# Two token sums moved into the projections, layer 2's first block sums moved behind two branch products, and first expert weight pieces asked for in another order

## The reference, cut to what matters

```python
def mixer_projections(h, w_in_l, q_norm_l, k_norm_l):
    z = jnp.einsum('bnd,de->bne', h, w_in_l)
    u_f, q_g, k_g, v_g, q_d, k_d, v_d, gates = jnp.split(z, _split_points(), axis=-1)
...
def merge_branches(u_f, o_g, o_d, gates, w_f, w_go, w_do, w_out):
    g_f, g_g, g_d = jnp.split(jax.nn.sigmoid(gates), N_BRANCHES, axis=-1)
    merged = (g_f * (fourier_mix(u_f) @ w_f)
              + g_g * (o_g @ w_go)
              + g_d * (o_d @ w_do))
    return merged @ w_out
...
    for l in range(DEPTH):
        h = modulate(rms_norm(x, norm1_g[l]), sh1, sc1)
        ...
        x = x + g1[:, None, :] * merge_branches(u_f, o_g, o_d, gates, w_fourier[l],
                                                w_gqa_o[l], w_diff_o[l], w_out[l])
        h = modulate(rms_norm(x, norm2_g[l]), sh2, sc2)
        x = x + g2[:, None, :] * moe(h, w_router, router_bias, w_e_gate[l], w_e_up[l], w_e_down[l])
```

## Time and profile before

| | us |
|---|---|
| three timed executions | 1937.16, 1942.76, 1942.72 (median 1942.72) |
| profiled execution, its own time | 1943.26 |
| its span, first to last instruction | 1941.2 |
| around the span | 2.06 |
| PE busy in the span | 1726.5 (89%) |
| DVE, ACT, POOL busy | 957.3, 718.6, 501.9 |
| TensorE clock granted, mean | 0.957 of full |

### The profile page before, as it was taken

The page is one execution under the profiler, slowest core; times in us unless marked ns, Lnnn a source line. Parts: engine busy times, 40 slices in busy tenths (PEclk is TensorE's granted clock), DMA queues, the critical chain, the costliest instruction groups (busy, mean ns, idle before and its releaser), DMA issues. The chain is left out here.

```text
span 1941.2 us, 34689 instructions
## 1 busy us (share of the span) xinstructions
PE 1726.5 (89%) x13363; PEld 1351.5 (70%) x13363; DVE 957.3 (49%) x1849; ACT 718.6 (37%) x1394; POOL 501.9 (26%) x268
## 2 busy tenths in 40 slices
PE   5999999989999987788689998888899999588893
PEld 4899866679999974222188997567899998432222
DVE  4285476785667333111283744766766652611114
ACT  4443465553433421111254434656433342211113
POOL 1303410065456302000101123201545551200004
PEclk8999999999999988999789999999999999899996
DMA  7512377823522337987442221001232340889744
GB/s 275 195 44 68 106 249 248 275 94 129 192 91 88 143 143 298 360 303 261 143 147 98 67 67 36 1 2 44 66 98 66 98 145 21 354 311 393 278 136 174
DMA packets 170647, 305.95 MB, mean 158 GB/s; under 512 B 12530, under 2 KB 123250, under 8 KB 169716
## 3 DMA queue, kind: packets, MB, share of 16 engines
q1 hardware_dynamic: 151248, 249.09, 37.1%
q10 hardware_dynamic: 13476, 33.67, 4.8%
q0 software_dynamic: 5760, 20.97, 2.9%
HBM read 517.87 MB, written 41.68 MB: 288 GB/s over the span
## 5 line engine op out<-in xcount | busy, mean ns | idle before, releaser
L2422 PE MATMUL psum<-xw,h_T 128*32 128x512 f32 x1792 | 209.3, 611 | 36.0 <-DMA xw<-w_expert 32.4
L181 PE MATMUL psum<-whi,h_hi 128*128 128x256 f32 x720 | 210.1, 292 | 0.5 <-ACT v_tok L1011 0.5
L817 POOL TENSOR_TENSOR wlo<-raw,whi 128x2048 fp32r<-128x2048 f32 x25 | 115.2, 4608 | 362.3 <-ACT whi L897 362.3
L181 PE MATMUL psum<-whi,h_lo 128*128 128x256 f32 x720 | 203.5, 283 | 0.0
L181 PE MATMUL psum<-wlo,h_hi 128*128 128x256 f32 x720 | 203.5, 283 | 0.0
L2422 PEld LDWEIGHTS psum<-xw,h_T 128*32 128x32 f32 x1792 | 53.9, 111 | 170.5 <-issue 113.5
L977 ACT ACTIVATE prob<-psum,small_stats 128x640 f32<-128x640 f32 (+1 forms) x160 | 112.0, 705 | 134.5 <-DVE small_stats L1380 134.3
L1380 DVE TENSOR_REDUCE small_stats<-psum 128x1 f32<-128x640 f32 (+1 forms) x160 | 107.3, 712 | 96.7 <-PE psum L1684 72.2
L2319 DVE TENSOR_TENSOR gated_x<-psum,sig_x 128x256 f32<-128x256 f32 x28 | 11.9, 425 | 279.9 <-ACT sig_x L2066 279.9
L181 PEld LDWEIGHTS psum<-whi,h_hi 128*128 128x128 f32 x720 | 137.5, 191 | 3.0 <-issue 1.8
L181 PEld LDWEIGHTS psum<-wlo,h_hi 128*128 128x128 f32 x720 | 137.9, 192 | 0.0
(11 more groups left out here) (375 smaller groups left out, 4108.3 us busy)
## 6 DMA issues: line engine op xcount, KB each, us to landing
xw<-w_expert SPq DMA_DIRECT2D x672, 512.0 KB
raw<-w_in SPq DMA_DIRECT2D x46, 1024.0 KB, 5.4
wm_rest<-w_mod SPq DMA_DIRECT2D x40, 1024.0 KB, 5.3
y_rows<-y_sel ACTq DMA_DIRECT2D x108, 128.0 KB, 5.2
h_sel<-h_rows ACTq DMA_DIRECT2D x22, 512.0 KB, 6.9
wm<-w_mod SPq DMA_DIRECT2D x4, 2048.0 KB, 16.1
raw<-w_out SPq DMA_DIRECT2D x8, 1024.0 KB, 5.2
h_rows<-c_zero ACTq DMA_DIRECT2D x4, 1536.0 KB, 8.9
```

The costliest lines, as they stand in the source:

```text
L181: mm = pe.matmul(dst, st, mv[q], start=start and n == 0, stop=stop and n == 2)
L817: pool.tensor_tensor(wlo[i % 2][:, :, :], raw[i % 2][:, :, :], whi[i % 2][:, :, :].bitcast(F32), ALU.subtract).then_inc(w_lo, 1)
L2422: mm = pe.matmul(psum[list_rows(q), i % 2, :], hT[i % 2][:, kc, q, :], xw[q][c][:, k * 512:(k + 1) * 512], start=(kc == 0), stop=(kc == KD ...
```

## The change

It moves instructions; none is added or removed.

A. SP stores `x_kept` after `stream(2)` instead of after `stream(4)`.

B. POOL's five steps of f_1 and f_2 stand behind `lo(3)` and ahead of `lo(6)`, the two low parts of s_1 and s_2 behind `lo(6)` and ahead of `lo(7)`. ACT's `sum_high(0)` and `sum_high(1)` stand ahead of units z(5, 1) and z(5, 3) instead of in attention steps 12 and 13.

C. Layer 2: POOL starts f_3 only when DVE has scaled the differential attention's rows (`d_3`). DVE's first four block sums and the three steps of s_4 stand behind the gate products of branch chunks 0 and 1, and s_4's low part behind that of chunk 3. ACT's `sum_high(2)` stands behind all seven `block_hi` of the first chunk. Layer 1: `sum_high(2)` stands behind `keep_diff` and ahead of the last five `block_hi`, not right behind `pw_high(0)`.

D. SP's pieces for the first expert tile: 7 at `g_pfree` 24 (before 4), 4 more at `o_full` 6, 11 at `o_full` 8 (before 18), 2 at `k_d` as before.

```diff
@@ sync
                     for i in range(2, N_WIN + (1 if first else 2)):
                         stream(i)
-                        if i == 4:
+                        if i == 2:
@@ gpsimd
+                    def first_sums():
+
+                        pool.wait_ge(n_lo, KD if first else 2 * KD)
+                        pool.wait_ge(x_moved, 16)
+                        add_up(f_1[1], f32(h_21[0]), f32(h_22[0]), ALU.add)
...
                         lo(i)
...
+                        if i == CH_KVG - 1:
+                            first_sums()
+                        if i == CH_QD + 1:
+                            for n, s in enumerate((s_1, s_2)):
+                                pool.wait_ge(a_hi, n + 1)
+                                pool.tensor_tensor(s[1], (f_1, f_2)[n][1], f32(s[0]), ALU.subtract).then_inc(a_lo, 1)
+
+                    if not first:
+                        pool.wait_ge(d_3, DH)
                     pool.wait_ge(t_o, NA)
@@ scalar
                     for n, u in enumerate(units):
+                        if u in (("z", CH_QD, 1), ("z", CH_QD, 3)):
+                            sum_high(u[2] // 2)
...
-                        if i in (12, 13):
-                            sum_high(i - 12)
...
                         pw_high(0)
-                        sum_high(2)
...
                     block_hi(n0, 0)
                     block_hi(n0, 1)
                     keep_diff()
-                    for j in range(2, 7):
-                        block_hi(n0, j)
+                    if first:
+                        sum_high(2)
+                        for j in range(2, 7):
+                            block_hi(n0, j)
+                    else:
+                        for j in range(2, 7):
+                            block_hi(n0, j)
+                        sum_high(2)
@@ vector
+                            if not first and g == 1:
+                                first_blocks()
+                            if g == (0 if first else 3):
                                 dve.wait_ge(a_hi, 4)
@@ sync, experts
+                    EARLY = [(c, 0) for c in range(N_PARTS + 1)] + [(2, 3), (3, 3)]
+                    LAST_STREAM = [(0, 2), (1, 2), (2, 1), (3, 1)]
+                    for c, q in EARLY:
+                        first_part(c, q)
+                    sp.wait_ge(o_full, KD - 2)
+                    for c, q in LAST_STREAM:
+                        first_part(c, q)
                     sp.wait_ge(o_full, KD)
```

More of the change, by code:

```diff
@@ L822, in _ @@
                             modulate_pool(pool, h_mix, kc)
[L823 to L826, removed]
                     n_step = [0]
@@ L837, in summed @@
                         pool.wait_ge(a_step, n)
[L839 to L843, removed]
-                    f32 = lambda x: x.bitcast(F32)
[L845 to L855, removed]
+                    f32 = lambda x: x.bitcast(F32)
+                    def first_sums():
+                        pool.wait_ge(n_lo, KD if first else 2 * KD)
+                        pool.wait_ge(x_moved, 16)
+                        add_up(f_1[1], f32(h_21[0]), f32(h_22[0]), ALU.add)
+                        add_up(f_1[0], f32(h_21[1]), f32(h_22[1]), ALU.add)
+                        summed(2)
+                        add_up(f_1[1], f_1[1], f_1[0], ALU.add)
+                        summed(3)
+                        add_up(f_2[1], f_1[1], f32(h_11[0]), ALU.subtract)
+                        summed(4)
+                        add_up(f_2[1], f_2[1], f32(h_11[1]), ALU.subtract)
+                    for i in range(2, N_WIN + n0):
+                        if i in (CH_KVG, CH_QD):
+                            continue
+                        lo(i)
+                        if i == CH_KVG - 1:
[6 more added lines that the diff above has]
+                        pool.wait_ge(d_3, DH)
                     pool.wait_ge(t_o, NA)
@@ L978, in exps, with sum_high @@
                                            accum_out=small[:, s, 1:2]).then_inc(t_exp, 1)
+                    def sum_high(n):
+                        s = (s_1, s_2, s_3, s_4)[n]
+                        act.wait_ge(a_step, (5, 5, SUM_STEPS, SUM_STEPS + 3)[n])
+                        act.activation(s[0], (f_1, f_2, f_3, f_4)[n][1], ACT.Copy).then_inc(a_hi, 1)
                     n_sqrt = 0
                     for n, u in enumerate(units):
+                        if u in (("z", CH_QD, 1), ("z", CH_QD, 3)):
+                            sum_high(u[2] // 2)
                         act.wait_ge(s_full, n + 1)
@@ L1040, in _ @@
                             exps(AHEAD[u])
[L1043 to L1047, removed]
                     def block_hi(n, j):
@@ L1962, in load_down @@
                                      bounds_check="skip_entire_dma").then_inc(xd_ld[h], 16)
-                    def first_down(q):
-                        for h in range(2):
-                            sp.dma_start(xw[q][N_PARTS + h][:, :], w_exp[N_PARTS + h, PER_LIST * q]).then_inc(xd_ld[h], 16)
                     def store_y(i, lists):
@@ L1977, in _ @@
                     low_ready(sp, N_STREAM - 1)
-                    for c in range(N_PARTS):
-                        for q in range(1, N_LISTS):
-                            sp.dma_start(xw[q][c][:, :], w_exp[c, PER_LIST * q]).then_inc(xw_ld[c], 16)
-                    for q in (0, 1, 3):
-                        first_down(q)
+                    rest = [(c, q) for c in range(N_PARTS) for q in range(N_LISTS)] + [(N_PARTS + h, q) for q in (0, 1, 3) for h in range(2)]
+                    for c, q in rest:
+                        if (c, q) not in EARLY + LAST_STREAM:
+                            first_part(c, q)
                     sp.wait_ge(k_d, TT)
-                    first_down(2)
+                    for h in range(2):
+                        first_part(N_PARTS + h, 2)
                     sp.wait_ge(k_t, KD)
```

25 lines of the change are left out of this document (13 added, 12 removed).

## The result

| | us |
|---|---|
| changed kernel, four executions | 1950.92, 1955.56, 1959.61, 1959.77 (median 1957.59) |
| kernel before, beside it | median 1942.22 |
| ratio, 95% interval | 1.0076 (1.0049 to 1.0104) |
| profiled execution, its own time and span | 1950.92, 1948.7 |
| PE, DVE, ACT, POOL busy | 1724.6, 954.7, 715.0, 510.4 |

What follows compares the result with a forecast made beforehand. PE, busy 89% of the span, was taken as the bound, others mattering only where it stands still. Terms -6.3 + 8.4 + 2.5 + 0.4 - 5.7 = -0.7 us gave 1942.0 us (own range 1938 to 1946; eight in ten 1932 to 1949.5).

Steps and rivals of the forecast that it cites:

- Attention: Attention with POOL's sums and low parts moved out: -5.0 us in layer 2, -1.3 in layer 1, together -6.3.
- Projections: Projections, where the moved POOL work makes DVE wait: +4.2 us a layer, +8.4 in all, bounds 0 and 17.
- The meeting of the fifth sum with one product: Projections: DVE's first product of chunk 2 waits 2.8 us for POOL; after slack of 1.1, PE loses 1.7 us.
- the second meeting: Projections: `lo(6)`, two low parts and `lo(7)` hold DVE's rotary products of rows (5,1) to (5,3); PE loses 2.5 us.
- the first rival: Projections absorb the sums, as DVE's products don't wait or slack exceeds 1.1 us: 1933.6 us, chance 0.29.
- Merge, layer 2: Layer 2's merge: PE's 4.60 us wait for `pw_lo` goes, a 5.0 us wait for POOL's low part comes: +0.4 us.
- Merge, layer 1, its start: Layer 1's merge: late `sum_high(2)` delays POOL's low parts and PE's block products: +2.5 us, bounds 0.5 and 3.5.
- Experts: First expert tile: earlier pieces let the last scatter land sooner, shortening PE's wait for `h_sel`: -2.5 and -3.2, together -5.7 us.
- the third rival: Experts stay as they were, since the scatters' own traffic sets the last landing: 1947.7 us, chance 0.10.
- The step that failed, first: Projections: SP's earlier store of `x_kept` delays two chunks of `w_in` by 12 us: counted as nothing, up to 2 us.
- The step that failed, second: Layer 1's merge: beyond the +2.5 us counted there, nothing in that layer gives anything back for it.
- the port lost at `lo(7)`: Projections: `lo(7)` takes the port ahead of row (5,2)'s last product: +7.4 us, 1949.4 us, chance 0.12.

Runs made afterwards that it cites:

- the first run: The changed kernel with the store of `x_kept` put back behind `stream(4)`, all else kept: ratio 1.0105 to the kernel before, median 1960.93 us.
- the eighth run: The kernel before with only layer 2's piece of part C (its merge) changed: ratio 0.9997 to the kernel before, -0.6 us.
- ninth run: The kernel before with layer 1's `sum_high(2)` late and, in both layers, each `pw` chunk asked for ahead of the raw chunk: ratio 1.0004.
- the sixth run: The changed kernel, in layer 1 storing `x_kept` behind `stream(3)` after ACT's small loads landed, and `sum_high(2)` right behind `pw_high(0)`: ratio 1.0010, median 1940.68 us.

## Why the prediction was wrong

The steps one by one, with what the trace of after gives:

- **Attention.** Layer 2 -4.4 of -5.0 forecast, layer 1 -0.5 of -1.3 (what runs on POOL there is `lo(11)`; layer 1 has no `lo(12)`). The mechanism held; the low parts of layer 1 gave less than those of layer 2, whose number was borrowed.
- **Projections.** Layer 1 +1.5 and +2.1 (forecast 1.7 and 2.5), layer 2 +3.8 (4.2). The meeting of the fifth sum with one product, its 2.8 us, the slack, and the second meeting all came close to what was worked out. This was the step on which the first rival stood: the products do wait. The Trainium skill's rule ("SBUF — State Buffer", "Who interferes with whom") was the right one to follow, and the rows of 2.80 and 5.84 us now show it for products with two inputs in this stage; the first run shows such waits for a `TENSOR_SCALAR` of four columns (2.57 us) and a copy (2.85) as well.
- **Merge, layer 2.** +0.3 (0.4), with a wait of 5.21 where 5.0 was forecast. Held, and the run of this piece alone agrees.
- **Merge, layer 1, its start.** +1.9 (2.5). Held.
- **Experts.** -0.8 by the run of the pieces alone, -1.6 and -1.2 in the trace of after, against -5.7. The premise failed that the pieces were in the scatters' way: in layer 2 it took 7.8 us after (1699.99 to 1707.81) and 8.6 before (1684.96 to 1693.58) from the last scatter's issue to SP's `h_sel` load, not about 6. This was the third rival. The wait for `h_sel` can't be read by itself: it fell from 5.62 to 3.08 us in layer 1 with the pieces alone, but to 2.77 and 2.03 in the eighth and ninth run too, which keep the old order, because PE had waited longer for `h_T` just ahead. The two waits together are 6.5 and 7.7 us (layers 1 and 2) in the mean of the six traces with the old order, and 5.7 and 6.4 in the mean of the eight with the new one: a gain of 0.8 and 1.3 us.
- **The step that failed, first.** "SP's earlier store of `x_kept` ... nothing, up to 2 us." I had asked only which chunks of `w_in` stand behind the store on SP's queue. The loads that suffered are issued by another engine, ACT, and DVE waits for them until 67.60 us: +7.9 in the trace, 7.6 by the run of the store alone. That row was in the trace of before with 9.95 us of waiting for `lam_in`; it is the place where layer 1's start has no slack. The Trainium skill says, in "DMA: Bandwidth & Descriptors", "Issuing engines are not separate DMA queues", that SP's and ACT's transfers go through the same engines; the trace agrees, with 12.4 us for a load that took 7.1.
- **The step that failed, second.** "Nothing in layer 1 gives anything back for it" stopped at the merge's first chunk. The delay doesn't stay 1.9 us; through SP's order of loads it puts the stage on its slower course: 5.5 us. The prediction named what waits behind POOL on PE, and not who waits for POOL's low parts on SP.

A third term was mis-sized, the experts' -5.7, which measured -0.8. With the failed steps put in, 7.9 + 5.5 + 1.9 + 3.6 + 3.8 - 0.5 - 4.4 + 0.3 - 0.8 = 17.3 us, where the medians differ by 15.4. By the experiments: store alone 7.6, late high part alone 5.6, everything else 1.9 (the sixth run): 15.1. The slower rival that I had named, the port lost at `lo(7)`, did not come, and that was luck: in layer 2 the last product of row (5,2) started at 1128.79, 0.24 us ahead of `lo(7)`. For parts B, C in layer 2 and D together, "about no change" is what the sixth run shows, but not by the forecast's terms (-3.2): attention gave less (-4.9 of -6.3) and the projections cost less (+7.4 of +8.4), which nearly cancels, and the experts' -5.7 did not come.

## What to carry to other kernels

When a transfer is moved, list every transfer that is in flight at its new time, on all queues, and who waits for each; here a 128 KB load with a waiting engine behind it cost 7.6 us, and a 1 MB chunk of `w_in` that the same store made land 6.9 us later was still there in time. An instruction that is moved on one engine is followed until the chain is back at PE: who waits for it, who waits for that, and which load stands behind the waiting one on SP. And work that blocks another engine is best moved to where that engine is idle, not to where its own engine is: POOL was idle in both places, but only behind `lo(10)` was DVE idle too.

## What the runs showed of the hardware

A single `TENSOR_SCALAR` of 128x4 took 2.57 us beside a POOL sum of 2.96. Maxima out of PSUM (`TENSOR_REDUCE`, 0.49 us for two of 128 columns) ran beside the sums at their usual length. When DVE started first, POOL waited in turn: a low part of 1.30 us took 2.29 beside DVE's `pw_lo`. I had not expected that a stage bound by PE could have two steady courses, 4.8 to 5.7 us apart in the five traces that show the slower one, and that in the eighth run 0.13 us between the starts of a DVE and a POOL instruction is where they part. What sets the landing time of the last scatter at the experts is open: with seven pieces fewer beside it, SP's load behind it left only 0.5 us sooner in layer 1 and 0.8 in layer 2 (means of the eight and six traces), and no run here changed the scatters themselves.
